# The second causal attention of a two-stack kernel: memory tasks first, the compressed branch beside them, its values opening the pair banks, slope tables on GpSimd

## The reference, cut to what matters

```python
def block(c):                                   # 128 queries of 512
    s_c = einsum(qb, kc) * scale - m * dist_c   # 31 compressed keys
    p_c = masked_softmax(s_c, cmp_end[None, :] <= tq[:, None])
    o_c = einsum(p_c, vc)
    ...                                         # s_s, s_w: full-length causal scores minus m * distance
    o = gb[..., 0:1] * o_c + gb[..., 1:2] * o_s + gb[..., 2:3] * o_w
o_mem = memory_attention(q_mem, mem, w_mem_kv)  # 4 heads over 256 memory rows
mix = concatenate([o_tok, o_mem]) @ w_out
```

## Time and profile before

| | us |
|---|---|
| median of 3 runs | 3189.24 (3189.17 to 3189.56) |
| the profiled execution, device time | 3191.15 |
| its span in the trace | 3189.4 |
| PE busy | 3021.9 (95%) |
| DVE, ACT, POOL busy | 1295.6, 1048.1, 139.1 |
| chain that ended last | PE 86%, DVE 8%, ACT 2%, rest 4% |

### The profile page before, as it was taken

The page is one execution under the profiler, slowest core; times in us unless marked ns, Lnnn a source line. Parts: engine busy times, 40 slices in busy tenths (PEclk is TensorE's granted clock), DMA queues, the critical chain, the costliest instruction groups (busy, mean ns, idle before and its releaser), DMA issues.

```text
span 3189.4 us, 36596 instructions
## 1 busy us (share of the span) xinstructions
PE 3021.9 (95%) x15462; PEld 2516.9 (79%) x15462; DVE 1295.6 (41%) x1859; ACT 1048.1 (33%) x1808; POOL 139.1 (4%) x214
## 2 busy tenths in 40 slices
PE   8999989999999899999889999899999978999998
PEld 6888878888888788887668888688888854688886
DVE  3463243333326532325654332423332558553224
ACT  3323234443444322213642222113221237522221
POOL 1000010030001000001000000100000100010000
PEclk9999999999999999999999999999999979999999
DMA  5333222232221223223112332432233410122321
GB/s 194 125 102 105 93 93 67 86 94 86 82 77 47 96 90 104 93 95 100 40 40 80 99 99 93 108 106 93 93 96 102 116 40 1 40 80 93 106 93 66
DMA packets 135010, 280.06 MB, mean 88 GB/s; under 512 B 20378, under 2 KB 33098, under 8 KB 134720
## 3 DMA queue, kind: packets, MB, share of 16 engines
q1 hardware_dynamic: 125232, 247.17, 24.1%
q0 software_dynamic: 9616, 30.57, 3.0%
HBM read 271.30 MB, written 4.25 MB: 86 GB/s over the span
## 4 chain that ended last, share of the span: by engine, by line
PE 86%; DVE 8%; ACT 2%; issue 2%; DMA 1%; POOL 1%; SPq 0%; DVEq 0%; POOLq 0%; ACTq 0%
PE bank L528 24%; PE bank L530 24%; PE bank L529 24%; PE bank L681 2%; PE bank L660 2%; PE bank L714 2%; PE bank L539 1%; PE bank L542 1%; PE bank L541 1%; PE bank L733 1%; PE bank L669 1%; PE bank L722 1%; PE bank L641 1%; DVE n_p L1623 1%; DVE x_rows L1554 1%
## 5 line engine op out<-in xcount | busy, mean ns | idle before, releaser
L1492 DVE TENSOR_TENSOR w_low<-raw,w_high 128x2048 fp32r<-128x2048 f32 (+2 forms) x221 | 499.9, 2262 | 1303.4 <-ACT w_high L1135 1297.1
L528 PE MATMUL bank<-xt_high,w_high 128*128 128x512 f32 x1984 | 779.6, 393 | 3.7 <-DVE w_low L1492 3.3
L530 PE MATMUL bank<-xt_high,w_low 128*128 128x512 f32 x1984 | 773.8, 390 | 0.0
L529 PE MATMUL bank<-xt_low,w_high 128*128 128x512 f32 x1984 | 773.2, 390 | 0.0
L1135 ACT ACTIVATE w_high<-raw 128x2048 fp32r<-128x2048 f32 (+2 forms) x221 | 417.5, 1889 | 991.1 <-PE bank L530 991.1
L528 PEld LDWEIGHTS bank<-xt_high,w_high 128*128 128x128 f32 x1984 | 372.5, 188 | 81.3 <-DVE w_low L1492 3.8
L530 PEld LDWEIGHTS bank<-xt_high,w_low 128*128 128x128 f32 x1984 | 372.4, 188 | 79.8
L529 PEld LDWEIGHTS bank<-xt_low,w_high 128*128 128x128 f32 x1984 | 372.7, 188 | 75.8
L528 PE MATMUL bank<-w_high,hidden_high 128*128 128x512 f32 x704 | 277.1, 394 | 3.1 <-DVE gate_rows L1821 3.1
L529 PE MATMUL bank<-w_low,hidden_high 128*128 128x512 f32 x704 | 275.7, 392 | 0.0
L530 PE MATMUL bank<-w_high,hidden_low 128*128 128x512 f32 x704 | 275.4, 391 | 0.0
(11 more groups left out here) (327 smaller groups left out, 3902.8 us busy)
## 6 DMA issues: line engine op xcount, KB each, us to landing
raw<-in_ffn_w_gu SPq DMA_DIRECT2D x80, 1024.0 KB, 5.1
raw<-in_ffn_w_down SPq DMA_DIRECT2D x44, 1024.0 KB, 5.0
raw<-in_b_w_in SPq DMA_DIRECT2D x40, 1024.0 KB, 5.2
raw<-in_a_w_in SPq DMA_DIRECT2D x24, 1024.0 KB, 5.2
raw<-in_a_w_out SPq DMA_DIRECT2D x8, 1024.0 KB, 5.0
raw<-in_ffn_w_gu SPq DMA_DIRECT2D x16, 512.0 KB, 4.4
raw<-in_w_out SPq DMA_DIRECT2D x5, 1024.0 KB, 5.0
raw<-in_w_mem_kv SPq DMA_DIRECT2D x4, 1024.0 KB, 5.2
```

The lines of the kernel that those rows point to most:

```text
L528: pe.matmul(o, lh, rh, start=start, stop=False, skip_group_check=True)
L529: pe.matmul(o, lh, rl, start=False, stop=False, skip_group_check=True)
L530: return pe.matmul(o, ll, rh, start=False, stop=stop, skip_group_check=True)
L1492: dve.tensor_tensor(homes[n][1][:, 0:w], RAW[n % 2][:, 0:w], homes[n][0][:, 0:w].bitcast(F32), ALU.subtract).then_inc(sem["w_low_ready"], ...
```

## The change

In order of the program:

- PE makes the compressed scores before the gates product, and DVE works on them in two halves of two tiles (768 columns) instead of four tiles. Masked keys are no longer multiplied by a 0/1 mask after the exponential; the row maximum is held at NEG/2 at least, so they come out as zero.
- ACT does the two exponentials of the compressed branch after the sigmoid and before its next `prepare`. The gates' turning, the sums, the scaling with the gate, the turning of the probabilities and its copy become `compressed_beside` callbacks inside `attend_pairs("nsa")`, at steps u = 1 and 3 to 6 on PE, slots 4 and 6 on DVE, slots 1, 7, 9, 11 and 13 on ACT.
- `nsa_tasks` puts the 16 memory tasks first.
- The compressed values are no longer multiplied ahead, copied out and added: when a pair's bank is opened, PE writes four matmuls of the compressed branch into it (start on the first), and the V matmuls add to that. Lines 1943, 1944 and 1641 of before are gone, as is the wait on `pair_summed`; the high and low parts read the bank.
- The slope tables are built by POOL, two instructions each (times slope, plus mask), one cell ahead; DVE waits for `slopes_ready` at slots 16, 32, ...
- DVE scales in pairs, in both attentions: at odd slots n it takes one reciprocal of two sums and scales tasks n-3 and n-2, where before each slot n took one reciprocal and scaled n-2.

The diff, cut to its core:

```diff
@@ nsa_tasks @@
         out = []
+        opened.clear()
+        mem_tasks(out, nQM, nKV)
         for i in range(HEADS // 2):
...
-        return mem_tasks(out, nQM, nKV)
+        return out
@@ PE, attend_pairs @@
+                    compressed = name == "nsa" and tasks[a]["pair"] < HEADS // 2
+                    if compressed and tasks[a]["opens"]:
+                        i = tasks[a]["pair"]
+                        for t in range(TT):
+                            pe.matmul(ps[tasks[a]["bank"]][:, t * P:t * P + P], VBD[:, i % 2, :], nCT[:, t, i // 2, :],
+                                      start=t == 0, stop=False, skip_group_check=True)
...
+                if beside:
+                    beside(u)
@@ PE, behind nsa_b @@
-        for t in range(TT + 1):
-            if t < TT:
-                pe.wait_ge(sem["cmp_p_ready"], at("cmp_p_ready", t))
...
+        product("nsa_gates", 8, [(ps[4][0:36, :], gate_operands)], lambda j: None)
         pe.wait_ge(sem["nq_read"], at("nq_read", ("b", 3)))
+        pe.wait_ge(sem["cmp_biased"], at("cmp_biased", TT - 1))
+        pe.wait_ge(sem["mem_kv_back"], at("mem_kv_back", 1))
+
+        def compressed_beside(u):
+
+            if u == 1:
+                pe.wait_ge(sem["gates_t_read"], at("gates_t_read"))
...
+            if 3 <= u < 7:
+                t = u - 3
+                pe.wait_ge(sem["cmp_p_ready"], at("cmp_p_ready", t // 2))
+                if t:
+                    pe.wait_ge(sem["cmp_pt_copied"], at("cmp_pt_copied", t - 1))
...
+        attend_pairs("nsa", compressed_beside)
@@ ACT @@
+        for half in range(2):
+            act.wait_ge(sem["cmp_shifted"], at("cmp_shifted", half))
+            act.activation(nCP[:, 2 * half:2 * half + 2], nCP[:, 2 * half:2 * half + 2],
+                           ACT.Exp).then_inc(sem["cmp_exp"], step("cmp_exp", half))
...
         prepare(ids["nsa_gates"][-1] + 2)
-        attend_pairs("nsa")
+        attend_pairs("nsa", compressed_beside)
@@ DVE, attend_pairs @@
-                        for g in range(2):
-                            ins = dve.scalar_tensor_tensor(out=nAB[2 * (i % 2) + g][:], in0=nDI[:],
-                                                           scalar=-slopes[6 * g + i] / HD_SCALE, in1=nCM[:],
-                                                           op0=ALU.mult, op1=ALU.add)
-                        link(ins)
+                    if name == "nsa" and n >= 16 and n % 16 == 0:
+                        dve.wait_ge(sem["slopes_ready"], at("slopes_ready", n // 16 - 1))
...
-                    link(dve.reciprocal(rd, DS[:, m % 8:m % 8 + 1]))
...
-                    dve.tensor_tensor(nOC[:, j, :], ps[tasks[n - 8]["bank"]][:], nOC[:, j, :],
-                                      ALU.add).then_inc(sem["pair_summed"], step("pair_summed", j))
+                if n % 2 and 3 <= n < N + 3:
+                    dve.wait_ge(sem["exp_done"], at("exp_done", (name, n - 2)))
+                    c = (n - 3) % 8
+                    link(dve.reciprocal(RD[:, c:c + 2], DS[:, c:c + 2]))
+                    for m in (n - 3, n - 2):
@@ POOL @@
+        for i in range(HEADS // 2):
+            if i == 0:
+                pool.wait_ge(sem["product_done"], at("product_done", ("panel", ids["nsa_a"][1])))
+            if i == 1:
+                pool.wait_ge(sem["cmp_p_turned"], at("cmp_p_turned", TT - 1))
+            if i >= 2:
+                pool.wait_ge(sem["masked"], at("masked", ("nsa", 16 * i - 1)))
+            for g in range(2):
+                ab = nAB[2 * (i % 2) + g][:]
+                link(pool.tensor_scalar(ab, nDI[:], -slopes[6 * g + i] / HD_SCALE, None, ALU.mult))
+                ins = pool.tensor_tensor(ab, ab, nCM[:], ALU.add)
+            ins.then_inc(sem["slopes_ready"], step("slopes_ready", i))
```

More of the change, by code:

```diff
@@ L449, in row_task @@
                   pair=pair, opens=o == 0 and t == 0 and first, closes=o == 64 and t == TT - 1 and last)
+        if tk["opens"]:
+            opened.append(pair)
+        tk["behind"] = opened[-3] if tk["opens"] and len(opened) > 2 else None
         out.append(tk)
@@ L734, in attend_pairs @@
                                             PTs[m % 4][:, i * P:(i + 1) * P],
-                                            start=tk["first"] and i == 0, stop=tk["last"] and i == parts - 1)
+                                            start=tk["first"] and i == 0 and not compressed,
+                                            stop=tk["last"] and i == parts - 1, skip_group_check=compressed)
                             if i == parts - 1:
                                 ins.then_inc(sem["weighted"], step("weighted", (name, m)))
+                if beside:
+                    beside(u)
         def turn_half(c, t):
@@ L1092, in _, with gate_operands @@
             ins.then_inc(sem["cmp_scored"], step("cmp_scored", t))
[L1093 to L1096, removed]
+        def gate_operands(kk, k, wh, wl):
+            return wh[:, 36 * kk:36 * kk + 36], wl[:, 36 * kk:36 * kk + 36], XTH[:, k, :], XTL[:, k, :]
+        product("nsa_gates", 8, [(ps[4][0:36, :], gate_operands)], lambda j: None)
@@ L1605, in attend_pairs @@
             for n in range(N + 9):
+                if beside:
+                    beside(n)
                 if n < N:
@@ L1962, in _, with half_of, over_keys @@
-        keep(TT - 1)
+        def half_of(cols, half):
+            return cols[:, 24 * half:24 * half + 24]
+        def over_keys(cols, half):
+            return half_of(cols, half).rearrange("p (h n) -> p h n", n=1).to_broadcast([P, 2 * HEADS, NC])
+        for half in range(2):
+            p = nCP[:, 2 * half:2 * half + 2].rearrange("p t h n -> p (t h) n")
+            for t in (2 * half, 2 * half + 1):
+                dve.wait_ge(sem["cmp_scored"], at("cmp_scored", t))
+                dve.scalar_tensor_tensor(out=nCP[:, t], in0=ps[t][:, 0:384].rearrange("p (h n) -> p h n", h=HEADS),
+                                         scalar=HD_SCALE, in1=nBC[:, t, :, :], op0=ALU.mult,
+                                         op1=ALU.add).then_inc(sem["cmp_biased"], step("cmp_biased", t))
+            dve.wait_ge(sem["cmp_biased"], at("cmp_biased", 2 * half + 1))
+            link(dve.tensor_reduce(half_of(CMAX, half), p, AX.X, ALU.max))
+            link(dve.tensor_scalar(half_of(CMAX, half), half_of(CMAX, half), NEG / 2, None, ALU.max))
+            dve.tensor_tensor(p, p, over_keys(CMAX, half), ALU.subtract).then_inc(sem["cmp_shifted"], step("cmp_shifted", half))
@@ new lines, in compressed_beside @@
+        def compressed_beside(n):
+            if n not in (4, 6):
+                return
+            half = (n - 4) // 2
+            p = nCP[:, 2 * half:2 * half + 2].rearrange("p t h n -> p (t h) n")
+            dve.wait_ge(sem["cmp_exp"], at("cmp_exp", half))
+            link(dve.tensor_reduce(half_of(CSUM, half), p, AX.X, ALU.add))
+            link(dve.tensor_scalar(half_of(CSUM, half), half_of(CSUM, half), 1e-30, None, ALU.max))
+            link(dve.reciprocal(half_of(CWGT, half), half_of(CSUM, half)))
+            dve.wait_ge(sem["ngates_read"], at("ngates_read"))
+            w = half_of(CWGT, half).rearrange("p (t h) -> p t h", t=2)
+            link(dve.tensor_tensor(w, w, nG[:, 2 * half:2 * half + 2, :, 0], ALU.mult))
+            dve.tensor_tensor(p, p, over_keys(CWGT, half), ALU.mult).then_inc(sem["cmp_p_ready"], step("cmp_p_ready", half))
```

169 lines of the change are left out of this document (55 added, 114 removed).

## The result

The changed kernel takes 3167.16 us (median of four runs, 3165.11 to 3173.55), 0.9933 of the time before, with a 95% interval of 0.9915 to 0.995. The forecast was 3161.1, the range 3149 to 3177. The profiled execution took 3165.86 us, its span is 3164.1, 25.3 shorter than before.

The account below looks back on a forecast made before the run. PE bounds the first attention; in the second, engines wait for each other behind a serial chain. Gains of 28.1 us until the first mask and 5.0 after, less 5.0 for POOL: 3189.2 - 28.1 = 3161.1 us, range 3149 to 3177.

Parts of the forecast that it names:

- Until the first mask: Ahead of the second attention: ACT's chain to the high part ends last; first mask at 2579.3 against 2607.44, gain 28.1 us.
- Memory tasks and compressed branch: Start of the second attention: 16 memory tasks 16.5 us, compressed branch 4.5, filling 0.5; token masks start 21.5 us later.
- The cell: Second attention, 16 tasks: 21.73 less 2.1 for tables and 0.68 for the addition, plus 0.86 for compressed matmuls: 19.8 us.
- in the second attention I take nothing for it: Paired reciprocals and scalings: counted as 0, bounds 0 and 1.5 us a cell, since T also waits for ACT's copy.
- First cell: First 16 token tasks of the second attention: 17.9 us, 1.9 less than other cells because its PE steps carry W = 256 tails.
- POOL beside DVE: Second attention: POOL's tables take 5.4 us an episode and slow DVE by 1 us in each of five, loss 5.0 us.
- if the scalings' mean rises by more than 0.1 us: Sign on DVE's scalings in the attention: a mean rise above 0.1 us would show the forecast wrong.
- rival 3: PE's clock stays at 1.2 GHz into the second attention's cells, about 33 us each; with all six, 3240 us; chance 0.04.
- clock low only between about 2575 and 2590: Sign: PE's clock drops only around its wait for the first mask and early memory tasks, then comes back.
- Rival 1: Each of 20 POOL instructions beside the attention stops DVE for its whole length: 22 us more, 3183 us; chance 0.08.
- Rival 2: Second attention's cells fall to what PE needs, some 17.8 us, without contention: 15 us less, 3146 us; chance 0.07.
- The first attention: PE is the bound there; pairs counted as 0, between a gain of 2 and a loss of 2.5 us.

Follow-up runs that it names:

- e6: Changed kernel with GpSimd building only the first pair of tables, ahead of the attention, used by all six cells; 3157.9 us, 0.9888 of the time before.
- e3: Changed kernel with one reciprocal and one scaling for each task instead of pairs, in both attentions; 3177.7 us, 0.9958 of the time before.
- e2: Changed kernel with GpSimd building only the tables of the first two cells, which later cells use again; 3162.9 us, 0.9918 of the time before.
- e11: Changed kernel with each GpSimd table instruction split into four of 224 columns; 3157.1 us, 0.9893 of the time before.
- e13: Changed kernel with the mask subtracted from the distances once, ahead of the attention, each table one whole multiplication; 3157.6 us, 0.9889 of the time before.

## Why the prediction was right or wrong

**Until the first mask**: right, 28.8 for 28.1, by the chain that was named. ACT's high part set the end, as said.

**Memory tasks and compressed branch**: e6 shows them undisturbed, 20.72 for 21.5. Right. The two halves of DVE's work put 2.63 us each in front of a mask, for the forecast's 2.8.

**The cell**: 19.91 without contention for 19.8, but four terms were off and cancelled, which is luck. The tables gave 1.5 instead of 2.1, the addition, by the remainder, 0.1 to 0.2 instead of 0.68: work on the chain of waits was priced at its full length, while part of it lay in slack that the chain does not show. The matmuls cost 0.68 for 0.86. And "in the second attention I take nothing for it" was wrong for the pairs: 0.84, inside the bound of 1.5. The reason given, that ACT's copy decides anyway, is the step that failed: PE's wait for that copy went from 1.8 to 0.4 us. Without pairs the cells would have been longer than before (23.42 in e3, 21.73 before).

**First cell**: 19.25 undisturbed for 17.9, 1.3 short. **Last cell and drain**: 17.94 and 8.34 for 18.5 and 7.6. First mask to `w_out` without POOL: 145.9 for 144.7.

**POOL beside DVE**: the mechanism right, the size half. POOL's work was priced at 5.4 us an episode and took 9.2; what it cost, 1 us an episode in the forecast, measured 1.37 in a cell, and 5.1 in the one that lies in the memory tasks and the first cell, 10.2 in all for 5.0. The bound of 0 to 27 held. The forecast's sign of error, "if the scalings' mean rises by more than 0.1 us", was met: 128x512 took 0.943 us on average instead of 0.546. What was missed is where a short stall weighs most: in a thin pipe, two stalls of 2.5 and 1.9 us starve PE, and the clock falls again, which was rival 3's mechanism in small (6.8 us at the lower clock, by the stretches 2600 to 2608). So the sign "clock low only between about 2575 and 2590" failed, though by 2610 the clock was back. Rival 1 did not decide: masks were not stopped (128x512 took 0.689 us in the mean in after and in e2, 0.693 at most), and of four instructions an episode two hold for 0.7 us at most. Rival 2 fell in e6: without contention the pipe stayed at 19.91 us a cell, not 17.8.

**The first attention**: 0.96 us gained, inside the bound of 2, by pairs. The rest of the 2.8 us ahead of the stage is not the change's: from the first attention's `w_out` to the compressed scores the eleven builds with the new order, alike in that stretch, take 920.2 to 923.5 us, and after's profile is the 920.2.

In the profiles 28.1 thus became 25.3: 5.2 us more contention and 1.2 of small terms, against 0.7 from the start, 1.0 from the pairs in the first attention, and 1.9 that vary between executions. The timed medians differ by 22.2 (3189.4 in these runs, 3167.2), near the 23.4 that are left when that last item is not there.

## What to carry to other kernels

Work that an engine does beside a busy pipe has to be priced by how long one instruction holds a shared resource, and at the place where the pipe is thinnest; cut into short pieces, or with its two-input half dropped, it cost nothing in the cells here. A step on the chain of waits is worth its length only if everything parallel to it is shorter by as much: here two tables of 2.17 us on DVE were worth 1.4 in the new order and 1.5 in the old. When a sum comes out right, undo the parts one at a time all the same: here four terms missed and cancelled.

## What the runs showed of the hardware

- A GpSimd addition of two 128x896 tiles (2.09 us) held a VectorE scaling until its end (2.31 us for 0.546 at 512 columns); a multiplication by a constant of the same tile (2.45 us) held one for up to 0.7, at its start or at its end, and let those that began 0.75 to 1.5 us in pass undisturbed. VectorE's masks, which read PSUM, kept their time beside both (0.693 us at most for 128x512).
- Four GpSimd pieces of 224 columns cost 0.77 us each in the multiplication and 0.66 in the addition, 3.1 and 2.65 for whole instructions of 2.45 and 2.09: the pieces are paid for on the engine that has room.
- The granted clock, at 1.00 again in 2590 to 2600, fell a second time, to 0.53 in 2600 to 2604, behind 4 us with PE busy 1.82; in e6, e11 and e13, without whole additions beside the memory tasks, it did not.
- The first attention's scores start up to 12 us apart in kernels that are the same up to there, and the 920 us between the attentions vary by 3.3; the first attention repeats to 0.02 us in the builds with pairs, and `w_out` to the end to 0.3.
